# A decoder layer with expert retrieval: its token blocks regrouped from 1, 3 and 4 to 1, 2, 3 and 2, and its expert rows buffered one by one

## The chip, the cores and the metric

One core of a Trainium2 chip runs the whole kernel. The metric is device time in microseconds (us), the median of several executions.

## What is computed

A prompt of 1024 tokens and 8 sample tokens go through one layer, with all weights in float32:

```python
n = rmsnorm(x, g_mix) * (1 + sc1) + sh1
z = n @ w_in                                   # 1024 -> 4096
a_lin, a_gate, u, v, g_a, g_b = split(z)
a = a_lin * sigmoid(a_gate)
a = silu(layernorm(causal_dwconv(concat(hist, a), w_dw, b_dw))) @ w_conv_out    # 31 taps
v = layernorm(v, g_v, b_v)
b = (u * chunk_spatial_gate(v, w_s, b_s)) @ w_gmlp_out
m = sigmoid(g_a) * a + sigmoid(g_b) * b
x = x + gt1 * (m @ w_out)
n2 = rmsnorm(x, g_ffn) * (1 + sc2) + sh2
# expert retrieval, per token: 8 heads, 16 of 16384 experts each
q = n2 @ w_q
s1, s2 = q[:half] @ k1.T, q[half:] @ k2.T      # top 16 of 128 each, then top 16 of their sums
act = gelu(u_tab[eid] . n2)                    # 128 rows of 1024 per token
x = x + gt2 * sum(g * act * v_tab[eid])        # 128 more rows of 1024 per token
y = rmsnorm(x, g_final)
```

## The kernel before

The prompt is 8 blocks of 128 tokens; the 8 samples are a ninth, narrow block. The work on a block has two halves. The **front** is everything up to the expert ids and gates: norm, input projection, gated units, convolution, layer norms, the branch products, the output projection, second norm, query product, top 16 searches, and **routing** (`route`), which picks a block's 128 experts per token and turns them into ids (`eid`) and gates. The **expert half** is the gather: a block has 64 **pairs** of slots. For each slot of a pair GpSimd issues one indirect DMA (`fetch`) that brings for each of 128 partitions one expert's row of 2048 numbers, u and v together, so a pair moves 2 x 1 MB. VectorE multiplies the u half with the token's norm and sums (`dots`, L1507), ScalarE takes the gelu (L987), VectorE makes a 128 x 32 weight matrix of it (`weigh`, L1524), and TensorE adds the v half, weighted, into the block's sums (`value`, L765), after which `rows_used` gives the rows' buffer back to GpSimd. There are 516 pairs: 64 for each block, and 4 for the samples ahead of the last block.

**Groups.** Fronts are done for several blocks at once, since each reads all weights (in pieces of 1 MB through `wring`, a ring of 3 pieces, loaded by the sync engine in order, L403 to L409). Group 1 is block 0, group 2 blocks 1 to 3 (384 tokens), group 3 blocks 4 to 7 with the samples (520 tokens, in two halves of 260 columns). Group 1's front runs by itself. Group 2's runs beside the expert pairs 0 to 59 of block 0, group 3's beside the pairs 64 to 247. Each group's last `route` calls for its later blocks are done beside the pairs just before those blocks (`extra` in the VectorE program): 10 steps each, one step per pair.

**What sets the order.** Each engine's front is a generator that yields at fixed points. `front_weights` lists the same points with a weight each, `spread_front` deals them out over the pairs of a range in proportion, and `beside_peer` walks through the pairs on every engine: the pair's dots, a few front steps, the pair's weigh or value, the other front steps. At a range's last pair the rest of the generator is run to its end. TensorE does half of a pair's front steps ahead of its value. All engines work in this order, so a late step of the front holds back the value behind it.

```python
for g, lo, hi in ((G2, 0, END_B), (G3, PAIRS, END_C)):     # 0 to 60, 64 to 248
```

**Row buffers.** `buffer_plan` gives each pair a slot of two rows (16 KB per partition): three slots up to pair 255 (`WIDE_AT`), five after it, when parts of `big`, `w1` and `arena` that the fronts need have come free. GpSimd waits once per pair for the `rows_used` of the pair that had the slot.

Of the kernel before, what the change touches and what calls it, by code (L numbers as in the profile page):

```python
# [20 lines left out]
D = 1024  # L21
NP = 1024
NS = 8
# [5 lines left out]
W = 31  # L29
# [15 lines left out]
NB1 = 4  # L45
GW = 520
# [9 lines left out]
END_B = 60  # L56
END_C = 4 * PAIRS - 8
WIDE_AT = 4 * PAIRS
# [58 lines left out]
def build(nc, t):  # L117
# [3 lines left out]
    with ctx:  # L121
# [10 lines left out]
        big = sb("big", [P, 6 * 2 * D + KC * GW])  # L132
        nT = part(big, 6 * 2 * D, KC, GW)
# [3 lines left out]
        mbuf = sb("mbuf", [P, KC * GW])  # L137
        mT = part(mbuf, 0, KC, GW)
        wring = sb("wring", [P, RING * PIECE])

        AW = 512 + W - 1
        arena = sb("arena", [P, CC * (AW + 2 * GW) + 5 * DC])
        aT = part(arena, 0, CC, AW)
        yT = part(arena, CC * AW, CC, GW)
        v_tm = part(arena, CC * (AW + GW), 5, DC)
        uT = part(arena, CC * (AW + GW) + 5 * DC, CC, GW)
        ysq = part(arena, CC * (AW + GW), CC, GW)
        x_first = part(arena, CC * AW, 5, D)
        eq = part(arena, CC * AW + 5 * D, 2, TOP, NC)
        xn2 = part(arena, 3768, 5, D)  # L150
        xn1 = sb("xn1", [P, NB1, D])
        xr = sb("xr", [P, NQ, D])
        v16 = part(arena, 0, 5, NCH, TOP)
        i16f = part(arena, 5 * NCH * TOP, 5, NCH, TOP)
        i16 = i16f.bitcast(u32)
        rep = part(arena, 10 * NCH * TOP, 4, NKEY)
# [5 lines left out]
        rbc = w1[:, 2048:2048 + GW]  # L162
        xs = part(w1, 0, 2, D)
        qbuf = part(w1, 0, 2, GW)
        qs = part(w1, 2 * GW, NCH, NS)
        rep_s = part(w1, 2 * GW + NCH * NS, 4, NKEY)
# [45 lines left out]
        def row(r):  # L212
            if r < 8:
                return big[:, r * 2 * D:(r + 1) * 2 * D]
            return w1[:, 0:2 * D] if r == 8 else arena[:, 0:2 * D]
# [15 lines left out]
        S = {f"{n}{g}": ctx.enter_context(nc.semaphore(f"{n}{g}")) for n in group_names for g in (1, 2)}  # L231
        S |= {f"{n}{g}": ctx.enter_context(nc.semaphore(f"{n}{g}")) for n in ("x_in", "out_x1") for g in (1, 2, 3)}
# [6 lines left out]
        s_row = [ctx.enter_context(nc.semaphore(f"rows{i}")) for i in range(10)]  # L239
# [5 lines left out]
        def group(n, blocks, tg, xn, tables):  # L245
# [6 lines left out]
            g.S = {k: S[f"{k}{1 if n < 3 else 2}"] for k in group_names}  # L252
            g.S |= {k: S[f"{k}{n}"] for k in ("x_in", "out_x1")}
            g.base = totals(G1) if n == 2 else {}

            g.order = list(range(g.nb)) if n < 3 else [0, 1, 2, 4, 3]
            g.cand = part(tables, 0, g.nb * H, NC)
            g.cid = part(tables, g.nb * H * NC, g.nb * H, NC)
            g.posf = part(mbuf, 3200, g.nb * H, TOP) if n < 3 else part(mbuf, 0, g.nb * H, TOP)
            g.crep = part(mbuf, 3200 + 512, H, NC) if n < 3 else part(mbuf, 1024, H, NC)  # L260
            g.eq = eq if n < 3 else part(mbuf, 2048, 2, TOP, NC)
            g.gt1 = (gt1_a, gt1_b, gt1_c)[n - 1]
# [5 lines left out]
        GROUPS = (G1, G2, G3)  # L268
        before = {2: G1, 3: G2}

        def cols(b):
            i = 0 if b == 0 else b - 1 if b < NB1 else b - NB1
            return slice(i * P, i * P + width(b))
# [115 lines left out]
        def x1_again(b):  # L389
            return mbuf[:, b * D:(b + 1) * D] if b < NB1 else wring[:, (b - NB1) * D:(b - NB1 + 1) * D]  # L390
# [1301 lines left out]
```

## Time and profile before

| what | value |
|---|---|
| median of 3 runs | 3551.34 us (3548.37 to 3553.54) |
| the profiled execution | 3556.78 us |
| its span | 3555.2 us |
| TensorE busy | 2051.7 us (58%) |
| VectorE busy | 2448.6 us (69%) |
| GpSimd busy | 1249.4 us (35%) |
| ScalarE busy | 441.8 us (12%) |
| DMA | 1232.08 MB, mean 347 GB/s |

Shares of busy time are means over stretches with different limits, so the span has to be cut. The page's 40 slices show where the limits change, and windows cut at chosen pairs measure each stretch. A stretch in which the DMAs are full can't be made shorter by faster engines; one in which they are not is paced by the engine that the others wait for.

### The profile page before, as it was taken

Reading aid. Unit: us, or ns where it says so; the run is one execution under the profiler, and the core shown is the slowest. Engines: PE = TensorE matmul, PEld = TensorE weight load, DVE = VectorE, ACT = ScalarE, POOL = GpSimd, SP = SyncE. Lnnn points to the kernel's source line nnn. Section 1 sums busy time; section 2 is a strip of 40 time slices with the busy share of each in tenths; the row PEclk is TensorE's granted clock in tenths of the full one; section 3 lists DMA queues with packets and bytes.
Section 4 is the critical chain, followed back from the end, with each engine's and each line's share of the span. In section 5 each row is a group of like instructions: output and inputs, shape, how many; then the busy total and the mean of one; then the engine's idle time right before and its main releaser. Section 6 shows DMA issues by size and latency. Waiting matters only on the chain. (4 is left out here: it accounts for less than half of the span.)

```text
span 3555.2 us, 28830 instructions
## 1 busy us (share of the span) xinstructions
PE 2051.7 (58%) x9548; PEld 995.9 (28%) x9548; DVE 2448.6 (69%) x6290; ACT 441.8 (12%) x1031; POOL 1249.4 (35%) x1046
## 2 busy tenths in 40 slices
PE   6873878986277777778688623333343333355333
PEld 4762444643144344455345300000000000000000
DVE  1447574479898796655768997766866697656665
ACT  1121101011111110110211011101010101011100
POOL 0001221222233433333434334544454444445343
PEclk9886988998588888899799855555555555555555
DMA  7734756798579999899999869999999998998998
GB/s 297 311 144 166 301 207 260 272 358 318 220 283 360 363 334 371 329 383 419 395 410 406 345 251 401 375 422 422 368 417 421 422 386 354 421 421 341 423 421 343
DMA packets 183925, 1232.08 MB, mean 347 GB/s; under 512 B 30512, under 2 KB 31152, under 8 KB 36320
## 3 DMA queue, kind: packets, MB, share of 16 engines
q0 software_dynamic: 148608, 1082.20, 75.9%
q1 hardware_dynamic: 35168, 148.05, 10.6%
q8 instruction: 75, 1.23, 0.1%
q14 instruction: 74, 0.61, 0.0%
HBM read 1221.14 MB, written 9.02 MB: 346 GB/s over the span
## 5 line engine op out<-in xcount | busy, mean ns | idle before, releaser
L1045 POOL DMA_INDIRECT big<-in_experts,eid x920 | 1112.0, 1209 | 2081.9 <-PE ps L765 1620.4
L1507 DVE SCALAR_TENSOR_TENSOR big<-big,xr 128x1024 f32<-128x1024 f32 x920 | 1113.6, 1225 | 525.3 <-DMA big<-in_experts,eid 520.2
L765 PE MATMUL ps<-big,wd 128*32 128x512 f32 x3680 | 726.2, 873 | 1089.8 <-DVE wd L1524 1085.2
L530 PE MATMUL ps<-big,wring 128*128 128x260 f32 (+2 forms) x2400 | 644.9, 423 | 81.5 <-issue 56.3
L530 PEld LDWEIGHTS ps<-big,wring 128*128 128x128 f32 x2400 | 447.6, 201 | 318.7 <-issue 166.1
L765 PEld LDWEIGHTS ps<-big,wd 128*32 128x32 f32 x3680 | 85.0, 127 | 1591.0 <-DVE wd L1524 1535.7
L987 ACT ACTIVATE gel<-act 128x2 f32<-128x2 f32 x516 | 105.7, 205 | 2569.9 <-DVE big L1507 2322.8
L1524 DVE TENSOR_SCALAR wd<-mask,gel,gate 128x32 f32<-128x32 f32 x1024 | 275.1, 363 | 152.3 <-ACT gel L987 141.5
L765 PE MATMUL ps<-w,wd 128*32 128x512 f32 x208 | 100.3, 1061 | 174.7 <-DVE wd L1524 170.8
L1205 DVE SCALAR_TENSOR_TENSOR arena<-arena,wdw 128x128 f32<-128x128 f32 (+2 forms) x360 | 182.9, 572 | 0.0
L682 PE MATMUL ps<-wring,mbuf 128*128 128x256 f32 (+1 forms) x528 | 128.6, 400 | 11.6 <-DMA wring<-in_w_out 6.3
L682 PEld LDWEIGHTS ps<-wring,mbuf 128*128 128x128 f32 (+1 forms) x528 | 96.0, 186 | 54.7 <-issue 28.8
L530 PE MATMUL ps<-arena,wring 128*128 128x260 f32 (+1 forms) x384 | 107.1, 422 | 0.0
L1045 POOL DMA_INDIRECT w<-in_experts,eid x52 | 57.2, 1100 | 130.3 <-PE ps L765 126.3
L765 PE MATMUL ps<-arena,wd 128*32 128x512 f32 x208 | 100.3, 1061 | 0.0
L1507 DVE SCALAR_TENSOR_TENSOR arena<-arena,xr 128x1024 f32<-128x1024 f32 x52 | 63.7, 1226 | 50.6 <-DMA arena<-in_experts,eid 50.6
L765 PEld LDWEIGHTS ps<-w,wd 128*32 128x32 f32 x208 | 10.2, 140 | 264.8 <-DVE wd L1524 259.2
L530 PEld LDWEIGHTS ps<-arena,wring 128*128 128x128 f32 x384 | 71.5, 190 | 37.9 <-issue 15.1
L1507 DVE SCALAR_TENSOR_TENSOR w<-w,xr 128x1024 f32<-128x1024 f32 x52 | 63.7, 1225 | 19.8 <-DMA w<-in_experts,eid 19.5
L1507 DVE DVE_READ_ACCUMULATOR big<-big,xr 128x1 f32 x920 | 76.8, 84 | 0.0
L1045 POOL DMA_INDIRECT arena<-in_experts,eid x52 | 68.6, 1319 | 15.9 <-issue 15.9
L814 ACT ACTIVATE xr<-arena 32x1024 f32<-32x1024 f32 x64 | 67.5, 1055 | 1.5
(219 smaller groups left out, 1881.0 us busy)
## 6 DMA issues: line engine op xcount, KB each, us to landing
wring<-in_w_in SPq DMA_DIRECT2D x40, 1024.0 KB
wring<-in_w_q SPq DMA_DIRECT2D x19, 1024.0 KB
big<-in_experts,eid POOLq DMA_INDIRECT x920
wring<-in_w_ada SPq DMA_DIRECT2D x12, 1024.0 KB
wring<-in_w_out SPq DMA_DIRECT2D x9, 1024.0 KB
big<-in_w_ada SPq DMA_DIRECT2D x6, 1024.0 KB, 6.9
xr<-in_w_ada SPq DMA_DIRECT2D x6, 1024.0 KB, 8.8
big<-in_w_in SPq DMA_DIRECT2D x4, 1024.0 KB, 14.7
```

The source lines that it names most:

```text
L530: mm = mmul(out, piece(n)[:, c, col:col + P], src[:, c, gi * tg:(gi + 1) * tg], start=(c == 0), stop=(c == k - 1))
L682: mm = mmul(ps[0:w, 2 + i % 6, 0:256], mT[:, c, cols(b)], piece(n + col)[:, c, :], start=(c == 0), stop=(c == KC - 1))
L765: mm = mmul(ps[QUAD * j:QUAD * (j + 1), half, :], wd[:, 2 * (at % 4) + jj, :], row(2 * slot + jj)[:, D + 512 * h:D + 512 * (h + 1)], start ...
L814: made = ac(xr[QUAD * q:QUAD * (q + 1), j, :], xn[QUAD * j:QUAD * (j + 1), :], ACT.Copy)
L987: ac(gel[:, c:c + 2], act[:, c:c + 2], ACT.Gelu).then_inc(S["gelu"], 1)
L1045: gp.indirect_dma_start(row(r), None, t["experts"], bass.IndirectOffsetOnAxis(ap=index, axis=0)).then_inc(s_row[r], 16)
L1205: ins = v.scalar_tensor_tensor(out=y, in0=aT[:, c, kk:kk + g.np], scalar=wdw[:, c, kk:kk + 1], in1=y, op0=ALU.mult, op1=ALU.add)
L1507: last = v.scalar_tensor_tensor(out=row(r)[:, 0:D], in0=row(r)[:, 0:D], scalar=1.0, in1=x, op0=ALU.mult, op1=ALU.mult, accum_out=act[:, c: ...
L1524: last = v.tensor_scalar(wd[:, c, :], mask[:], gel[:, c:c + 1], gate[:, b % 4, 2 * half + jj, m:m + 1], ALU.mult, ALU.mult)
```

## The change

- The groups are now blocks 0; 1 and 2; 3 to 5; 6, 7 and the samples (`STARTS`). There is a fourth front, so all weights of a front are read once more. Each later front works on one column range: 256, 384 and 264 tokens.
- The fronts run beside pairs 0 to 59, 64 to 187 and 204 to 311 (`FRONT_AT`). The later routes run beside pairs 64 (group 2's), 192 and 202 (group 3's), 320 and 384 (group 4's: the samples' first, then block 7).
- The rows are kept singly: seven up to pair 319, ten after it. Each fetch waits for the pair that last used its own row. The seventh row is a tile of its own (`row7`), for which `mbuf` shrinks from 4160 to 3200 numbers.
- The tables, views and copies of x follow (group 3's x is loaded in group 2's time; blocks 3 to 5 are kept in `xn1`); the semaphores of the groups are shared by all, with a base count for each.

```diff
-NB1 = 4
-GW = 520
+STARTS = [0, 1, 3, 6]
+NB1 = STARTS[-1]
+NBL = NBT - NB1
+GT = (NBL - 1) * P + NS
+GX = 3 * P
+ROWS_1, ROWS_2 = 7, 10
+LAST = len(STARTS)
...
-END_B = 60
-END_C = 4 * PAIRS - 8
-WIDE_AT = 4 * PAIRS
+FRONT_AT = {2: (0, PAIRS - 4), 3: (PAIRS, 3 * PAIRS - 4), 4: (3 * PAIRS + 12, 5 * PAIRS - 8)}
+WIDE_AT = 5 * PAIRS
...
-    plan, uses, newest = [], [0] * 5, [None] * 5
+    plan, uses, newest = [], [0] * ROWS_2, [None] * ROWS_2
     for at in range(NPAIRS):
-        free = range(3 if at < WIDE_AT else 5)
-        slot = min(free, key=lambda i: -1 if newest[i] is None else newest[i])
-        plan.append((slot, uses[slot], newest[slot]))
-        uses[slot] += 1
-        newest[slot] = at
+        tiles = []
+        for _ in range(2):
+            free = range(ROWS_1 if at < WIDE_AT else ROWS_2)
+            r = min(free, key=lambda i: -1 if newest[i] is None else newest[i])
+            tiles.append((r, uses[r], newest[r]))
+            uses[r] += 1
+            newest[r] = at
+        plan.append(tiles)
...
-        big = sb("big", [P, 6 * 2 * D + KC * GW])
+        big = sb("big", [P, 6 * 2 * D + KC * GX])
...
+        row7 = sb("row7", [P, 2 * D])
+        mbuf = sb("mbuf", [P, 3200])
...
-        G1 = group(1, [0], P, xn1[:, 0:1, :], mbuf)
-        G2 = group(2, [1, 2, 3], 3 * P, xn1[:, 1:4, :], mbuf)
-        G3 = group(3, list(range(NB1, NBT)), 260, xn2, wring)
+        for n in range(1, LAST):
+            blocks = list(range(STARTS[n - 1], STARTS[n]))
+            GROUPS.append(group(n, blocks, len(blocks) * P, xn1[:, blocks[0]:blocks[-1] + 1, :], mbuf))
+        GROUPS.append(group(LAST, list(range(NB1, NBT)), GT, xn2, wring))
...
+        routing = [(PAIRS, ROUTE_PIECES, G2, 1), (3 * PAIRS, ROUTE_PIECES, G3, 1),
+                   (3 * PAIRS + ROUTE_PIECES, ROUTE_PIECES, G3, 2), (5 * PAIRS, ROUTE_PIECES + 1, G4, 1),
+                   (6 * PAIRS, ROUTE_PIECES, G4, 2)]
...
-                if earlier is not None:
-                    pool.wait_ge(S["rows_used"], earlier + 1)
                 for jj in range(2):
+                    r, _, earlier = PLAN[at][jj]
+                    if earlier is not None:
+                        pool.wait_ge(S["rows_used"], earlier + 1)
```

GpSimd's queue at its first fetches (`big` holds six rows, `row` is the seventh). Before:

```order
L1045 DMA big<-in_experts,eid 128x2048 [waits first_ids]
L1045 DMA big<-in_experts,eid 128x2048 x5
L1045 DMA big<-in_experts,eid 128x2048 [waits rows_used]
L1045 DMA big<-in_experts,eid 128x2048
L1045 DMA big<-in_experts,eid 128x2048 [waits rows_used]
L1045 DMA big<-in_experts,eid 128x2048
L1045 DMA big<-in_experts,eid 128x2048 [waits rows_used]
L1045 DMA big<-in_experts,eid 128x2048
```

and now:

```order
L1076 DMA big<-in_experts,eid 128x2048 [waits first_ids]
L1076 DMA big<-in_experts,eid 128x2048 x5
L1076 DMA row<-in_experts,eid 128x2048
L1076 DMA big<-in_experts,eid 128x2048 [waits rows_used] x7
L1076 DMA row<-in_experts,eid 128x2048 [waits rows_used]
L1076 DMA big<-in_experts,eid 128x2048 [waits rows_used]
L1076 DMA big<-in_experts,eid 128x2048 [waits rows_used,first_ids]
L1076 DMA big<-in_experts,eid 128x2048 [waits rows_used] x5
```

Every fetch has a wait of its own, seven are issued before the first of them, and the two fetches of a pair no longer wait for the same pair.

TensorE in block 0, at the third and the later pairs of group 2's input projection (four L765 rows are a pair's value; `wring` holds the weight pieces). Before:

```order
L530 MATMUL ps<-big,wring 128x384 x24
L765 MATMUL ps<-big,wd 32x512 x4
L530 MATMUL ps<-big,wring 128x384 x12
L765 MATMUL ps<-big,wd 32x512 x4
L530 MATMUL ps<-big,wring 128x384 x16
L765 MATMUL ps<-big,wd 32x512 x4
L530 MATMUL ps<-big,wring 128x384 x12
L765 MATMUL ps<-big,wd 32x512 x4
```

and now, with the line numbers of the new file (L562 and L797 are L530 and L765):

```order
L562 MATMUL ps<-big,wring 128x256 x16
L797 MATMUL ps<-big,wd 32x512 x4
L562 MATMUL ps<-big,wring 128x256 x16
L797 MATMUL ps<-big,wd 32x512 x4
L562 MATMUL ps<-big,wring 128x256 x8
L797 MATMUL ps<-big,wd 32x512 x4
L562 MATMUL ps<-big,wring 128x256 x12
L797 MATMUL ps<-row,wd 32x512
```

About as many matmuls lie beside each pair as before, but each has 256 columns instead of 384.

TensorE around pair 256. Before, 20 pairs of values follow each other behind the end of group 3's front (its last row is L736), and more after them:

```order
L736 MATMUL ps<-ident,mod 8x128 x8
L765 MATMUL ps<-big,wd 32x512 x80
L765 MATMUL ps<-w,wd 32x512
L765 MATMUL ps<-arena,wd 32x512
L765 MATMUL ps<-w,wd 32x512
```

and now group 4's output projection lies between them (L714; the rows with 8 are the samples'):

```order
L701 MATMUL ps<-ident,mod 8x128
L797 MATMUL ps<-row,wd 32x512
L797 MATMUL ps<-big,wd 32x512
L797 MATMUL ps<-row,wd 32x512
L797 MATMUL ps<-big,wd 32x512
L714 MATMUL ps<-wring,mbuf 128x256 x12
L797 MATMUL ps<-big,wd 32x512 x4
L714 MATMUL ps<-wring,mbuf 128x256 x4
L714 MATMUL ps<-wring,mbuf 8x256 x4
L797 MATMUL ps<-big,wd 32x512 x4
L714 MATMUL ps<-wring,mbuf 8x256 x4
```

The values of block 4's pairs stand behind front work as those of the blocks before do.

## Rows read from the trace of the kernel before

**Rows 1.** The page: 40 slices of 88.9 us, busy tenths, clock, DMA share, GB/s
```profile
PE   6873878986277777778688623333343333355333
DVE  1447574479898796655768997766866697656665
PEclk9886988998588888899799855555555555555555
DMA  7734756798579999899999869999999998998998
GB/s 297 311 144 166 301 207 260 272 358 318 220 283 360 363 334 371 329 383 419 395 410 406 345 251 401 375 422 422 368 417 421 422 386 354 421 421 341 423 421 343
```

**Rows 2.** Windows at pairs: start, 0, 60, 64, 84, 232, 248, 256, 272, 320
```profile
core 0: us, PE busy (x) PEld busy (x) DVE busy (x) ACT busy (x) POOL busy (x), PEclk, DMA share, GB/s
...
304.60:914.30 609.70, 465.27 (x1824) 262.30 (x1824) 406.02 (x1160) 71.95 (x152) 142.52 (x120) 0.87 0.70 268
914.30:932.40 18.10, 6.27 (x28) 0.81 (x32) 11.44 (x25) 0.82 (x4) 6.84 (x6) 0.50 0.60 226
932.40:1092.00 159.60, 101.59 (x444) 61.13 (x440) 145.66 (x405) 22.78 (x53) 50.80 (x40) 0.75 0.74 282
1092.00:1994.80 902.80, 690.84 (x3360) 425.89 (x3353) 656.06 (x1591) 131.19 (x320) 355.84 (x297) 0.87 0.96 381
1994.80:2128.00 133.20, 42.63 (x206) 14.30 (x204) 126.79 (x494) 11.80 (x27) 42.88 (x34) 0.56 0.73 280
2128.00:2164.80 36.80, 14.00 (x60) 1.61 (x64) 23.55 (x50) 5.87 (x12) 19.04 (x18) 0.50 0.81 329
2164.80:2255.70 90.90, 30.48 (x128) 3.02 (x120) 81.86 (x212) 6.16 (x19) 39.24 (x31) 0.50 0.92 370
2255.70:2497.00 241.30, 93.29 (x388) 9.87 (x392) 146.44 (x291) 26.63 (x64) 115.05 (x98) 0.50 1.01 422
```

**Rows 3.** Groups of instructions, TensorE, 304.6 to 914.3 us: busy, mean ns, idle before
```profile
L530 PE MATMUL ps<-big,wring 128*128 128x384 f32 x704 | 248.8, 507 | 37.8 <-issue 18.6 <-DVE arena L1253 8.0 <-DMA wring<-in_w_in 7.2
L765 PE MATMUL ps<-big,wd 128*32 128x512 f32 x480 | 71.7, 673 | 93.5 <-DVE wd L1524 92.3 <-DVE xn L1341 1.0
```

**Rows 4.** Who waited for whom: GpSimd in 304.6 to 914.3, then 932.4 to 2128 us
```profile
POOL big L1045 <- PE ps L765: 429.2, 57, 25.5
...
POOL big L1045 <- PE ps L765: 659.6, 177, 17.8
```

**Rows 5.** Windows as above: a busy TensorE, the wait for weights, a routing burst
```profile
388.00:427.00 39.00, 39.00 (x166) 24.12 (x165) 29.66 (x62) 2.57 (x8) 15.22 (x10) 1.00 0.87 340
1525.00:1537.00 12.00, 0.06 (x1) 0.09 (x1) 4.18 (x9) 1.65 (x3) 0.00 (x0) 0.57 1.02 423
1537.00:1560.00 23.00, 23.00 (x108) 15.76 (x109) 9.77 (x22) 4.45 (x8) 8.73 (x8) 0.93 0.73 272
1601.30:1633.30 32.00, 26.21 (x120) 17.40 (x120) 13.29 (x28) 2.63 (x6) 9.00 (x8) 0.82 1.02 417
2096.00:2128.00 32.00, 1.94 (x8) 0.20 (x8) 31.04 (x54) 4.14 (x5) 3.05 (x2) 0.50 0.39 158
```

**Rows 6.** Timeline of GpSimd: start, duration, idle before: first, last of twelve, 23.5
```profile
964.17 0.94 POOL L1045 DMA_INDIRECT big<-in_experts,eid  x1 [8.02 <-PE ps L765]
...
2106.65 2.11 POOL L1045 DMA_INDIRECT big<-in_experts,eid  x1 [10.90 <-PE ps L765]
...
2133.49 0.94 POOL L1045 DMA_INDIRECT big<-in_experts,eid  x1 [23.49 <-PE ps L765]
```

**Rows 7.** Groups by form, VectorE, whole span: the convolution taps
```profile
L1205 DVE SCALAR_TENSOR_TENSOR arena<-arena,wdw 128x512 f32<-128x512 f32 x120 | 84.6, 748 | 0.0
L1205 DVE SCALAR_TENSOR_TENSOR arena<-arena,wdw 128x384 f32<-128x384 f32 x120 | 66.0, 614 | 0.0
L1205 DVE SCALAR_TENSOR_TENSOR arena<-arena,wdw 128x128 f32<-128x128 f32 x120 | 32.3, 355 | 0.0
```

**Rows 8.** Windows as above: pairs 320 to 335 with one route, 336 to 383
```profile
2497.00:2586.50 89.50, 30.52 (x128) 3.02 (x120) 81.92 (x213) 6.16 (x19) 38.93 (x31) 0.50 0.91 364
2586.50:2827.20 240.70, 93.25 (x388) 9.89 (x392) 146.40 (x291) 26.64 (x64) 114.78 (x98) 0.50 1.01 422
```

**Rows 9.** The page: the DMA queue of the sync engine, packets, MB, share
```profile
q1 hardware_dynamic: 35168, 148.05, 10.6%
```

More of the change, by code:

```diff
@@ L238, in build @@
         s_piece = [ctx.enter_context(nc.semaphore(f"piece{i}")) for i in range(RING_1)]
-        s_row = [ctx.enter_context(nc.semaphore(f"rows{i}")) for i in range(10)]
+        s_row = [ctx.enter_context(nc.semaphore(f"rows{i}")) for i in range(ROWS_2)]
         def width(b):
@@ L443, in _ @@
                         sp.dma_start(xn1[:, b, :], t["x"][b * P:(b + 1) * P, :]).then_inc(S["x_in2"], 16)
[L444 removed]
+            for n in range(first_piece[2], first_piece[3]):
+                if n == first_piece[2] + 4:
+                    for b in G3.blocks:
+                        sp.dma_start(xn1[:, b, :], t["x"][b * P:(b + 1) * P, :]).then_inc(S["x_in3"], 16)
                 with_spill(n, G2)
[L447 removed]
@@ L746, in value @@
                 b, half, m = place(at)
-                slot = PLAN[at][0]
+                rows = [row(tile[0]) for tile in PLAN[at]]
                 pe.wait_ge(S["weights"], at + 1)
@@ L775, in sample_x @@
                     mm = mmul(ps[:, pair(k) + half, :], ident[0:NS, k:k + 1].broadcast_to([NS, P]),
-                              xn2[0:NS, 4, 512 * half:512 * (half + 1)], start=True, stop=True)
+                              xn2[0:NS, SB, 512 * half:512 * (half + 1)], start=True, stop=True)
                 mm.then_inc(S["xb_mm"], 1)
@@ L786, in begin @@
                         made[0] += 1
-            beside_peer(begin, value, {2: front(G2), 3: front(G3)}, lambda at: None, share=0.5)
+            beside_peer(begin, value, {g.n: front(g) for g in GROUPS[1:]}, lambda at: None, share=0.5)
         @block.scalar
@@ L966, in front @@
                     ac(gts, bank2(6)[0:NS, :], ACT.Copy).then_inc(s["gt_done"], 1)
-                yield from gap(27 if g.n == 3 else 11)
+                yield from gap(19 if g.n == LAST else 11)
                 next(g.numerators)
@@ L1001, in root @@
                 ac(stat[:, 1, lo:hi], stat[:, 0, lo:hi], ACT.Sqrt).then_inc(S["fin_root"], 1)
-            exps = {PAIRS + ROUTE_PIECES * i + 6: G2 for i in range(2)}
-            exps |= {at + 6: G3 for at in (4 * PAIRS, 5 * PAIRS, 6 * PAIRS, 6 * PAIRS + ROUTE_PIECES + 1)}
+            exps = {start + 6: g for start, _, g, _ in routing}
             copies = {half_start(h - 1) + 20 + c: (h, c) for h in range(2, 2 * NB) for c in range(8)}
@@ L1017, in extra @@
                     root(1, 0, NB)
-            beside_peer(gelu, lambda at: None, {2: front(G2), 3: front(G3)}, extra)
+            beside_peer(gelu, lambda at: None, {g.n: front(g) for g in GROUPS[1:]}, extra)
             square(NB)
@@ L1595, in to_slots, with later_routes @@
                 yield
-            def routing_2():
-                for i in (1, 2):
-                    yield from route(G2, i)
-            def routing_3():
-                for i in range(1, 4):
-                    yield from route(G3, i)
-                yield from to_slots()
-                yield from route(G3, 4)
-            second, third, norms = routing_2(), routing_3(), early_norm()
-            def extra(at):
-                if PAIRS <= at < PAIRS + 2 * ROUTE_PIECES:
-                    next(second, None)
-                for b, count in ((4, ROUTE_PIECES), (5, ROUTE_PIECES), (6, 2 * ROUTE_PIECES + 1)):
-                    if b * PAIRS <= at < b * PAIRS + count:
-                        next(third, None)
+            def later_routes():
+                for _, _, g, turn in routing:
+                    yield from route(g, turn)
+                    if g.blocks[g.order[turn]] == NB:
+                        yield from to_slots()
+            routes, norms = later_routes(), early_norm()
+            def extra(at):
+                for start, count, _, _ in routing:
+                    if start <= at < start + count:
+                        next(routes, None)
                 if at - 2 in ends:
@@ L1619, in _ @@
             dve.wait_ge(S["mask_made"], 1)
-            beside_peer(dots, weigh, {2: front(G2), 3: front(G3)}, extra)
+            beside_peer(dots, weigh, {g.n: front(g) for g in GROUPS[1:]}, extra)
             take_acc(2 * NB)
```

193 lines of the change are left out of this document (101 added, 92 removed).

## The prediction

> **What bounds the kernel now.** I read the page's slices first [rows 1]: no engine is full over the span. VectorE and TensorE are busy but gapped in the first half, and in the second half the DMA share stands at 0.9 to 1.0 with 421 GB/s. The windows, cut at the moments at which a named pair of slots begins its dot products, give each stretch its own limit [rows 2]. With no front beside them, pairs 272 to 319 take 241.3 us for 48, that is 5.03 each, at 422 GB/s: a pair gathers 2.1 MB, so this is the DMA's own pace, about 4.98 us, and a block of 64 pairs can't take less than 319 us. Above that floor lies all that a schedule can change:
>
> - Pairs 0 to 63, with group 2's front (384 tokens) beside 60 of them: 609.7 + 18.1 = 628 us, 309 over the floor. TensorE is busy for 465.3 of the 609.7 us and VectorE for 406.0, while the DMAs give 268 GB/s [rows 2]. The value matmuls take 71.7 of TensorE's time, the front the rest [rows 3], and GpSimd waits 429 us for TensorE to give rows back [rows 4]. So TensorE's order bounds this stretch.
> - Pairs 64 to 319, with group 3's front (512 tokens and the samples) beside pairs 64 to 247: 1564.6 us. The floor is 1275, and the front's 33.6 MB of weights are 80 us more at 421 GB/s, so 210 us are lost. They go where routing makes VectorE the slowest (159.6 us for the first 20 pairs, 133.2 for pairs 232 to 247), and where the front stops for something [rows 2]. From the start to pair 0's dots, 304.6 us, nothing changes.
> - From pair 320, 2497 us, 1058 us to the end, mostly the floor.
>
> **What a stop costs.** In pairs 151 to 154 TensorE waits 14 us for two weight pieces. While it waits the DMAs run at 423 GB/s, so nothing is lost yet; the loss comes behind it, 23 us at 272 GB/s, since no rows had been given back. That is 8 us of DMA time [rows 5]. The routing burst at a front's last pair is larger: VectorE has 31 us of work in pair 247, and the DMAs fall to 158 GB/s for 32 us, 20 us lost; GpSimd stands still for 23.5 us in it [rows 5, 6].
>
> **The change part by part, against the profiled 3556.8 us (span 3555.2; the median of the runs is 5.4 lower).**
>
> 1. *Group 2 shrinks from three blocks to two.* In block 0, TensorE's front work goes to two thirds: 394 to 263 us, and with 72 us of values 335 instead of 465. The 144 us in which it idled are kept (479 us for 60 pairs) or shrink alike (431). But the DMAs now matter: 60 × 4.98 + 80 = 379 us, 6.3 per pair, so a light pair can no longer run at the 3 us of its dots. I went through the printed orders pair by pair, gave each instruction the mean duration of its form (half a matmul's time for half its columns), and added up, for each pair, the largest of TensorE's work, VectorE's work and the pair's DMA share. For the kernel before this gives 608 us where 609.7 were measured, so I go by it: after, it gives 507, and 20 for the last four pairs. **Block 0: 628 to 527, minus 101.** Ends: 449 and 560.
> 2. *Pairs 64 to 319 now hold two fronts*, group 3 with 384 tokens beside 124 pairs and group 4 with 256 and the samples beside 108. The columns that TensorE multiplies are the same as before, only moved, but three things are added. The weights are read once more: 80 us of DMA time in a stretch that is near the floor. The convolution's 120 tap instructions come once more: 614 and 748 ns for 384 and 512 columns [rows 7] make 163 us, and with groups of 256, 384 and 256 (a tap of 256 lies between the 355 and 614 ns of its neighbours, at 485) 190: 27 us more on VectorE. And the norms, softmax chains and burst at the end of a front come once more. The same pair-by-pair sum gives 1556 us for the kernel before (1564.6 measured) and 1708 after. **Plus 152.** From below: if the second front only cost its DMA time and took a third of block 0's work along, plus 80. From above: twice the 210 us lost now, and 80, plus 290.
> 3. *What such a sum can't see*: the two mid-branch waits for weight pieces in every front (8 us each, above) and the waits at its phase borders. Over group 3's front the measured time is 18 us above the sum (1195.6 against 1177). A third front repeats this: **plus 18** (0 to 40).
> 4. *Seven single row buffers beside the fronts instead of three pairs.* Half a pair more can be fetched before a stop empties the queue. The price is to be seen in routing: ten pairs of VectorE work at 7 us instead of 5 should cost 20 us, and do so with three pairs of buffers; with five they cost 10 (89.5 us against 16 × 4.98 = 80) [rows 8]. With three pairs of buffers the first 20 pairs of group 3's front, two routes among them, ran 51 us over their 5.42 each [rows 2]. So two pairs of buffers absorb 10 us, one row 2.5. Between pairs 64 and 247 GpSimd waits twelve times for over 8 us, the longest 17.8 [rows 4] but for the 23.5 above; I take these for nine stops, and 18 with two fronts: **minus 45**. In block 0 the rows wait for the engines anyway, and I take nothing. From below 0, from above 70 if block 0 gains too. Before, the waits for `rows_used` came once per pair; now each fetch has one, on an otherwise idle queue: nothing.
> 5. *Widening to ten rows at pair 320 instead of 256*: the two routes of group 3 (pairs 192 to 211) run with seven rows. This is inside term 2, which counts them at their full work.
> 6. *The end*: block 6 no longer holds two routes but one; by the same sum the rest from pair 320 to the last dots goes from 1035 to 1016: **minus 19**. The moved norm inputs, the smaller `mbuf` and the shared semaphores add no instruction on a path that is waited for: group 3's x is loaded one front ahead, and group 4's is asked for at group 3's last pair, 16 pairs before its use.
>
> Sum: −101 + 152 + 18 − 45 − 19 = **+5 us**. Carried to the median of the runs, 3551.3 + 5 = 3556.
>
> The Trainium skill (Perfetto Trace Analysis, Per-instruction lifecycle) says that VectorE's SBUF operations are slower than spec by a fixed cost per instruction, so that small operands suffer most. It speaks against smaller groups; the taps agree (355 ns at 128 columns, 748 at four times as many), and term 2 already pays it.
>
> **The rivals.**
>
> *Faster: block 0 shrinks in full.* Block 0 is where most was lost, and term 1's lower end is 78 us below what I take. If TensorE's idle shrinks with its work, the end is at 3556 − 78 = 3478. For it: GpSimd's 429 us of waiting there are all for TensorE [rows 4]. Against: where TensorE works without a gap (39 us at full clock), the DMAs already give 340 GB/s [rows 5]; with a third less work beside each pair they are the next bound.
>
> *Slower: the third front costs as much as the second did.* Its place is pairs 204 to 311, of which pairs 272 to 311 ran at 5.03 us with VectorE 61 per cent busy [rows 2]. My sum has 728 us for these 108 pairs, 6.7 each, 110 over gathers and weights (108 × 4.98 + 80 = 618). If group 4's front loses there what group 3's did, the 210 us less some 40 for two routes, the end is 60 later, at 3616. It decides from 7.3 us per pair. For it: bursts and waits for pieces come once per front, not per token. Against: group 3's front with twice the tokens ran at 6.5 per pair, routes included.
>
> *The seventh buffer does nothing.* In the wait for weights above the DMAs were full. A further gather in flight then only stands before the weights, and TensorE starts 2.5 us later for each row that came 2.5 us sooner. Then term 4 is nought: 3601. The Trainium skill (Trainium Kernel Development and Optimization, Key Constraints) says that DMAs issued from SP, ACT and POOL all run on the same 16 engines and interleave. By that rule the gathers and weights do delay each other, and the trace agrees: 417 GB/s together in a window with both [rows 5]. But behind such a wait the DMAs run dry, and there the row counts.
>
> **How the numbers follow.** A measurement can tell some 0.2 per cent, 7 us, from no change. The balance as summed: 0.50, 3520 to 3595 where each term errs by a fifth, of which 0.18 lie faster, 0.16 within 7 us, 0.16 slower. Block 0 in full: 0.27. The full third front: 0.12. The idle seventh row: 0.11. So faster 0.45, same 0.16, slower 0.39. The predicted time is the balance's, 3556. The range goes from the fast rival, 3475, to above the slow one, 3625; what lies outside are sums in which two rivals meet.
>
> **What would show it.** In the windows after: pair 64 begins its dots near 830 us instead of 932, and pair 320 near 2515 instead of 2497. Weight bytes rise by 33.6 MB, on a queue that moves 148 MB now [rows 9]; if not, the change doesn't do what it says. TensorE's busy time stays near 2050 us, VectorE's goes up by 30 to 40. DMA slices between 2160 and 2500 us fall from 420 to 340 GB/s. The stops of 14 us for weight pieces stand six times, not four. I'd be wrong by term 1 if block 0 ends before 790, by term 2 if pairs 64 to 319 take less than 1630 us or more than 1740, and by term 4 if pairs in routing bursts still lose what they did.

## The result and the profile after

| | kernel before | changed kernel |
|---|---|---|
| median, 14 runs each on one chip | 3547.64 us (3533.81 to 3553.54) | 3558.63 us (3547.98 to 3564.04) |
| ratio | 1 | 1.0033, 95% interval 1.0021 to 1.0045 |
| the profiled execution, its span | 3556.78, 3555.2 us | 3552.07, 3550.0 us |
| TensorE, VectorE busy | 2051.7, 2448.6 us | 2049.4, 2470.4 us |
| DMA | 1232.08 MB | 1264.60 MB |
| bytes on the sync engine's queue, which loads the weights | 148.05 MB | 180.56 MB |

The changed kernel is slower by 0.33 per cent, 11 us. The time that I named, 3556 us, is 2.6 us off, but it stood for a difference of 5 us, inside what a measurement can tell from no change, and the measured one lies 4 us outside (its interval is 7 to 16 us). The profiled executions scatter by more than this effect (by the two in the table the changed kernel would be 5 us faster, and a second profile of it has a span of 3569.9 us), so they are used for where the time lies, and the medians for how much it is.

The page of the changed kernel, slices of 88.8 us, its clock, DMA share and GB/s, and the sync engine's queue:

```profile
PE   6864877935867786862376677672343333354333
...
DVE  1456864798796556798968655689866585657665
...
PEclk9976988956978897975587888785555555556555
DMA  7836887968998899997779989995999999999998
GB/s 290 324 133 233 352 310 306 397 272 330 388 358 341 314 401 421 399 387 308 283 298 394 370 350 420 405 408 215 406 409 421 422 373 420 421 421 364 423 422 340
...
q1 hardware_dynamic: 39488, 180.56, 12.8%
```

Against the kernel before [rows 1], the fifth to ninth slices, in block 0, have risen from a mean of 280 GB/s to one of 327 (four of the five rose, the ninth fell), and the stretch near the floor now begins at the 29th slice instead of the 25th. Between 2160 and 2500 us there is a fourth front, with one slice at 215 GB/s, its last burst.

Windows of the changed kernel, cut at pairs 0, 60, 64, 192, 248, 256, 304, 320, 384, 448 and the end:

```profile
298.90:793.50 494.60, 345.87 (x1656) 236.80 (x1656) 348.64 (x996) 60.98 (x145) 136.69 (x117) 0.82 0.80 317
793.50:813.60 20.10, 8.21 (x36) 1.01 (x40) 12.09 (x26) 1.46 (x5) 10.79 (x10) 0.50 1.01 414
813.60:1657.90 844.30, 590.41 (x2376) 282.56 (x2368) 639.79 (x1686) 111.94 (x247) 304.43 (x256) 0.81 0.90 362
1657.90:2050.80 392.90, 222.59 (x988) 116.93 (x988) 315.25 (x775) 55.41 (x119) 140.64 (x112) 0.72 0.88 345
2050.80:2103.00 52.20, 38.76 (x177) 26.60 (x174) 26.99 (x59) 7.36 (x17) 14.58 (x14) 0.85 0.83 323
2103.00:2393.40 290.40, 217.67 (x1084) 127.07 (x1083) 204.29 (x608) 35.95 (x105) 112.24 (x98) 0.86 1.00 409
2393.40:2512.00 118.60, 29.67 (x132) 3.34 (x136) 105.32 (x359) 15.37 (x28) 38.20 (x35) 0.52 0.67 262
2512.00:2837.10 325.10, 123.77 (x516) 12.91 (x512) 224.23 (x480) 32.64 (x83) 152.04 (x128) 0.50 1.00 414
2837.10:3183.30 346.20, 129.12 (x525) 14.76 (x518) 228.56 (x503) 32.64 (x83) 153.79 (x130) 0.50 0.99 409
3183.30:3550.00 366.70, 152.07 (x572) 20.27 (x571) 230.36 (x446) 35.98 (x99) 157.98 (x126) 0.53 0.94 388
```

Block 0 took 514.7 us instead of 628 [rows 2], pairs 64 to 319 took 1698.4 instead of 1564.6, and from pair 320 to the end 1038 instead of 1058.2. So 113 us were won in block 0, 134 lost behind it, and 20 won at the end; the rest of the difference between the two profiles, 6 us, is the stretch before pair 0.

In finer stages (us between the dots of the pairs named, from the two profiles):

| pairs | before | after | what stands beside them now |
|---|---|---|---|
| 0 to 31 | 348 | 282 | group 2's projection and branches, 256 columns for 384 |
| 32 to 63 | 280 | 233 | its output projection, queries, routing |
| 64 to 187 | 818 | 829 | group 3's front, 384 columns for 512 |
| 188 to 203 | 86 | 95 | a route and the start of another, formerly front work |
| 204 to 311 | 620 | 740 | the rest of that route and group 4's front; formerly 44 pairs of front and a route |
| 312 to 319 | 41 | 35 | nothing |
| 320 to 383 | 330 | 325 | one route |
| 384 to the end of the last dots | 714 | 699 | one route instead of two |

Nearly all of the loss is in pairs 204 to 311. There the pace is 6.85 us per pair; the slow rival needed 7.3, my sum had 6.7.

The waits of the changed kernel, GpSimd for TensorE in block 0 and in pairs 64 to 319, then VectorE for rows in the latter stretch:

```profile
POOL big L1076 <- PE ps L797: 354.1, 56, 28.7
...
POOL big L1076 <- PE ps L797: 966.8, 239, 23.5
...
DVE big L1536 <- DMA big<-in_experts,eid: 316.4, 191, 13.4
```

GpSimd's waiting for TensorE beside pairs 0 to 59 fell from 429.2 us [rows 4] to 354.1, 75 us, while the stretch itself became 115 us shorter; the DMAs carry 317 GB/s there now instead of 268. Its longest wait behind block 0 is a routing burst of 23.5 us, exactly that of before [rows 6]:

```profile
2455.89 2.10 POOL L1076 DMA_INDIRECT big<-in_experts,eid  x1 [10.90 <-PE ps L797]
2458.30 0.94 POOL L1076 DMA_INDIRECT row<-in_experts,eid  x1 [0.30 <-issue]
2482.75 0.93 POOL L1076 DMA_INDIRECT big<-in_experts,eid  x1 [23.52 <-PE ps L797]
```

This is GpSimd's timeline at pair 311, group 4's last: the seventh row has been issued, at 2458.30, and the engine then waits as long as it did with six.

### The profile page after: what moved, and what is told of

Its sections match the earlier page's. It is cut to its first block, busy times and chain, and to the rows that moved or that the text cites. A ratio compares the mean times of both kernels' runs of the same rounds, so it can differ in the third digit from the quotient of the medians.

```text
span 3550.0 us, 29121 instructions
## 1 busy us (share of the span) xinstructions
PE 2049.4 (58%) x9564; PEld 1006.1 (28%) x9564; DVE 2470.4 (70%) x6457; ACT 449.5 (13%) x1042; POOL 1233.4 (35%) x1046
## 2 busy tenths in 40 slices
DMA packets 188247, 1264.60 MB, mean 356 GB/s; under 512 B 30992, under 2 KB 31632, under 8 KB 36544
## 3 DMA queue, kind: packets, MB, share of 16 engines
q1 hardware_dynamic: 39488, 180.56, 12.8%
## 4 chain that ended last, share of the span: by engine, by line
DMA 25%; DVE 13%; PE 9%; issue 5%; POOL 2%; ACT 1%; POOLq 0%; ACTq 0%; DVEq 0%
DMA big<-in_experts,eid 12%; DMA w<-in_experts,eid 12%; PE ps L562 4%; PE ps L797 4%; DVE big L1536 3%; POOL big L1076 2%; DVE wd L1553 2%; DVE eid_s L1499 1%; DVE mbuf L1497 1%; DVE arena L1497 1%; DVE arena L1494 1%; DVE mbuf L1494 1%; PE ps L807 1%; ACT gel L1019 1%; PE ps L714 0%
## 5 line engine op out<-in xcount | busy, mean ns | idle before, releaser
L1076 POOL DMA_INDIRECT big<-in_experts,eid x829 | 969.7, 1170 | 2178.2 <-PE ps L797 1754.3
L797 PE MATMUL ps<-big,wd 128*32 128x512 f32 x3316 | 806.9, 856 | 1039.3 <-DVE wd L1553 1035.3
L1536 DVE SCALAR_TENSOR_TENSOR big<-big,xr 128x1024 f32<-128x1024 f32 x829 | 1004.0, 1223 | 483.7 <-DMA big<-in_experts,eid 477.7
L562 PE MATMUL ps<-big,wring 128*128 128x256 f32 (+3 forms) x2400 | 671.3, 435 | 125.9 <-issue 79.9
L562 PEld LDWEIGHTS ps<-big,wring 128*128 128x128 f32 x2400 | 459.6, 206 | 381.0 <-issue 209.3
L797 PEld LDWEIGHTS ps<-big,wd 128*32 128x32 f32 x3316 | 94.0, 126 | 1529.8 <-DVE wd L1553 1472.1
L797 PE MATMUL ps<-row,wd 128*32 128x512 f32 x472 | 184.4, 869 | 127.0 <-DVE wd L1553 117.5
L1235 DVE SCALAR_TENSOR_TENSOR arena<-arena,wdw 128x256 f32<-128x256 f32 (+2 forms) x480 | 199.0, 478 | 0.0
L1536 DVE SCALAR_TENSOR_TENSOR row<-row,xr 128x1024 f32<-128x1024 f32 x118 | 144.1, 1221 | 58.1 <-DMA row<-in_experts,eid 57.6
L1076 POOL DMA_INDIRECT row<-in_experts,eid x118 | 147.0, 1245 | 36.0 <-issue 36.0
L714 PE MATMUL ps<-wring,mbuf 128*128 128x256 f32 (+1 forms) x528 | 130.9, 406 | 9.6 <-DMA wring<-in_w_out 6.5
L714 PEld LDWEIGHTS ps<-wring,mbuf 128*128 128x128 f32 (+1 forms) x528 | 98.3, 191 | 54.1 <-issue 27.3
L562 PE MATMUL ps<-arena,wring 128*128 128x256 f32 (+2 forms) x384 | 107.2, 422 | 0.0
L846 ACT ACTIVATE xr<-xn 32x1024 f32<-32x1024 f32 x96 | 101.1, 1053 | 2.0
L562 PEld LDWEIGHTS ps<-arena,wring 128*128 128x128 f32 x384 | 71.4, 190 | 37.4 <-issue 15.9
L797 PE MATMUL ps<-arena,wd 128*32 128x512 f32 x152 | 73.3, 1061 | 3.0 <-DVE wd L1553 3.0
L797 PEld LDWEIGHTS ps<-row,wd 128*32 128x32 f32 x472 | 20.9, 127 | 188.4 <-DVE wd L1553 160.9
L797 PE MATMUL ps<-w,wd 128*32 128x512 f32 x156 | 74.3, 1049 | 0.0
```

Source lines behind the costliest of these rows:

```text
L562: mm = mmul(out, piece(n)[:, c, col:col + P], src[:, c, gi * tg:(gi + 1) * tg], start=(c == 0), stop=(c == k - 1))
L714: mm = mmul(ps[0:w, 2 + i % 6, 0:256], mT[:, c, cols(b)], piece(n + col)[:, c, :], start=(c == 0), stop=(c == KC - 1))
L797: mm = mmul(ps[QUAD * j:QUAD * (j + 1), half, :], wd[:, 2 * (at % 4) + jj, :], rows[jj][:, D + 512 * h:D + 512 * (h + 1)], start=(m == 0), ...
L846: made = ac(xr[QUAD * q:QUAD * (q + 1), j, :], xn[QUAD * j:QUAD * (j + 1), :], ACT.Copy)
L1076: gp.indirect_dma_start(row(r), None, t["experts"], bass.IndirectOffsetOnAxis(ap=index, axis=0)).then_inc(s_row[r], 16)
L1235: ins = v.scalar_tensor_tensor(out=y, in0=aT[:, c, kk:kk + g.np], scalar=wdw[:, c, kk:kk + 1], in1=y, op0=ALU.mult, op1=ALU.add)
```

## The experiments

Each kernel was timed against the kernel before on the same chip; the kernels of one batch share its runs. The medians of the kernel before in the three batches are 3544.89, 3544.69 and 3545.74 us.

**The changed kernel again**, as the base of the first batch.

> The changed kernel once more, on the chip of the three beside it. Theory (the sum of the prediction): within 0.1 to 0.5 per cent slower than the kernel before, 3552 to 3565 us.

Measured: 3562.22 us (5 runs), ratio 1.0047 (1.0034 to 1.0061). Its stages agree with the first profile's within 8 us: block 0 took 520.6 us, pairs 64 to 319 1701.5, and the stretch from pair 320 to the end 1045.9. Below, the changed kernel stands as 3559 to 3562 us. Of the three batches it has runs in the first alone, so beside the kernels of the other two its ratios to the kernel before, 1.0033 and 1.0047, are the better base (a ratio and the quotient of the two medians differ by up to 0.0006).

**Six rows instead of seven**, the grouping alone:

```diff
-ROWS_1, ROWS_2 = 7, 10
+ROWS_1, ROWS_2 = 6, 10
```

> The changed kernel with six single row buffers beside the fronts instead of seven. My theory (a row absorbs 2.5 us of each of 18 stops): 45 us slower than the changed kernel, near 3603, all of it in pairs 64 to 319. Rival (the seventh buffer does nothing, since it only stands before the weights): within 7 us of the changed kernel.

Measured: 3642.73 us, ratio 1.0271 (1.0253 to 1.0290). The seventh row is worth 80 us by the medians and 65 to 85 by the profiles, and not 45. Windows of it, pairs 0 to 63 and 64 to 319, then 160 to 183, 184 to 191, 192 to 203:

```profile
302.10:839.30 537.20, 361.26 (x1692) 241.23 (x1696) 362.09 (x1020) 62.89 (x149) 142.32 (x126) 0.80 0.79 309
839.30:2594.70 1755.40, 1110.12 (x4752) 559.19 (x4748) 1293.95 (x3483) 225.97 (x516) 608.32 (x516) 0.77 0.88 346
...
1487.20:1644.70 157.50, 113.51 (x460) 52.40 (x460) 130.19 (x520) 13.99 (x40) 53.78 (x48) 0.80 0.91 350
1644.70:1713.40 68.70, 14.72 (x64) 1.62 (x64) 59.18 (x168) 8.72 (x15) 19.87 (x16) 0.50 0.65 258
1713.40:1793.20 79.80, 24.02 (x104) 2.41 (x96) 73.26 (x212) 5.31 (x15) 31.83 (x24) 0.50 0.83 323
```

and the last three stretches of the changed kernel:

```profile
1447.80:1592.00 144.20, 109.91 (x456) 52.12 (x460) 129.15 (x521) 14.03 (x40) 52.33 (x48) 0.83 0.96 389
1592.00:1657.90 65.90, 17.04 (x72) 1.62 (x64) 59.03 (x169) 8.79 (x16) 22.62 (x17) 0.50 0.67 262
1657.90:1737.70 79.80, 22.58 (x96) 2.43 (x96) 73.24 (x212) 5.31 (x15) 31.27 (x24) 0.50 0.84 334
```

Of the row's gain 17 to 22 us lie in block 0, where I had taken nothing, and 54 to 57 in pairs 64 to 319. Within those it isn't where I had put it. In pairs 160 to 183 it gains 13 us; in the routing burst and the route behind it, where I had read its price, 3 and 0. In pairs 160 to 183 a pair with 6.7 us of top 16 searches on VectorE is followed by one with 3.0 or 4.4, and TensorE's work too changes from pair to pair. Over the 24 pairs VectorE is busy for 129 us and TensorE for 110, both less than the 138 us for which the DMAs are busy (0.96 of 144.2), so it is the alternation that makes the DMAs wait. There the DMA share rises from 0.91 to 0.96. In the burst and the route behind it VectorE has more work than the DMAs for many pairs together (59 of 65.9 us and 73 of 79.8), and there one row more gained next to nothing. Nor did the row remove many stops: in pairs 64 to 319 GpSimd waits for over 8 us 29 times with six rows, and 27 and 28 times in the two profiles with seven.

What the row did take away are VectorE's waits for rows. With six, in pairs 0 to 63 and then 64 to 319:

```profile
DVE big L1536 <- DMA big<-in_experts,eid: 62.4, 37, 5.0
...
DVE big L1536 <- DMA big<-in_experts,eid: 389.2, 238, 11.2
```

and with seven, in the same two stretches (the last line is the seventh row's own):

```profile
DVE big L1536 <- DMA big<-in_experts,eid: 19.5, 20, 3.4
...
DVE big L1536 <- DMA big<-in_experts,eid: 316.4, 191, 13.4
DVE row L1536 <- DMA row<-in_experts,eid: 17.0, 14, 4.0
```

In pairs 64 to 319 these waits are 56 us shorter, as much as the stretch itself; in block 0 they are 43 us shorter, of which 17 to 22 show in the time.

**Five rows**, for the slope:

```diff
-ROWS_1, ROWS_2 = 7, 10
+ROWS_1, ROWS_2 = 5, 10
```

> The changed kernel with five single row buffers beside the fronts. My theory: each row less costs at least as much as the one before, so 100 us or more slower than the changed kernel. Beyond stops, five rows of 1 MB give 2.5 pairs in flight, and the loop of a pair took 18 us in pairs 128 to 191 of the kernel before, so 7.2 us per pair instead of 6.2 would give 250 us more. Rival: rows don't matter, below 30 us.

Measured: 3830.09 us, ratio 1.0805 (1.0791 to 1.0820), 268 to 271 us above the changed kernel. The sixth row is worth 187 us, the seventh 80. The expectation's 250 us, from the loop of a pair, came near: pairs 128 to 191 took 7.4 us each with five rows, where the loop gave 7.2, and 6.6 with six, 6.2 with seven.

**Rows kept singly in the kernel before**, six beside the fronts:

```diff
+ROWS_1, ROWS_2 = 6, 10
...
-        slot = min(free, key=lambda i: -1 if newest[i] is None else newest[i])
+            r = min(free, key=lambda i: -1 if newest[i] is None else newest[i])
...
-                if earlier is not None:
-                    pool.wait_ge(S["rows_used"], earlier + 1)
                 for jj in range(2):
+                    r, _, earlier = PLAN[at][jj]
+                    if earlier is not None:
+                        pool.wait_ge(S["rows_used"], earlier + 1)
```

> The kernel before with its six rows kept singly (and ten after pair 256), groups as they were. In even counts a pair's two rows still wait for the pair three ahead, so my theory: no change within 0.2 per cent. Rival (the single waits themselves help or cost on GpSimd): more than 7 us either way.

Measured: 3546.41 us (11 runs), ratio 1.0005 (0.9996 to 1.0014). Keeping rows singly does nothing by itself. The difference of the changed kernel is thus made of two parts: the groups, +98 us (3642.7 against 3544.9), and the seventh row, −80. The groups' part includes the widening to ten rows at pair 320 instead of 256, which no run takes out of it. The kernel before with a seventh row wasn't tried: the 8 KB per partition for the row are what `big` (4352 bytes) and `mbuf` (3840) give up with the narrower groups.

**The order of two weight pieces in every later front.** The sync engine loads the pieces in the order of their use. The twelfth and eighteenth of a front are the second output pieces of the two branches. Each has to wait for the ring place of a piece that TensorE uses long, the branch's first output piece, and the next input piece stands behind it in the queue, though its place is free sooner and it is wanted sooner. The two change places:

```diff
+            early = {}
+            for g in GROUPS[1:]:
+                for k in (11, 17):
+                    at = first_piece[g.n] + k
+                    early |= {at: at + 1, at + 1: at}
             def with_spill(n, g):
-                load(n)
+                load(early.get(n, n))
```

> The changed kernel, in whose later three fronts the sync engine loads the third input piece of a branch ahead of its second output piece, so that at mid-branch one piece of 1 MB is waited for and not two. Theory (term 3: a wait for pieces costs some 8 us of DMA time, six of them, half of each goes): 15 to 25 us faster than the changed kernel. Rival (these waits are covered by rows that wait for their dots anyway): within 7 us of the changed kernel (about 3560 us).

Measured: 3538.61 us (12 runs), ratio 0.9987 (0.9977 to 0.9997), 20 to 24 us below the changed kernel by the medians, 16 to 21 by the ratios. TensorE's waits ahead of its weight loads, of the changed kernel:

```profile
PEld ps L562 <- issue: 225.2, 187, 15.0
```

and with the order changed (L568 is the same line):

```profile
PEld ps L568 <- issue: 147.5, 189, 8.8
PEld ps L568 <- DMA wring<-in_w_conv_out: 28.4, 3, 9.6
PEld ps L568 <- DMA wring<-in_w_gmlp_out: 27.8, 3, 9.9
```

One of these stops, the second of group 3, in TensorE's timeline of the changed kernel and then of this one:

```profile
1222.60 5.14 PE L562 MATMUL ps<-big,wring 128*128 128x384 f32 x8 [13.72 <-issue]
...
1213.12 5.49 PE L568 MATMUL ps<-big,wring 128*128 128x384 f32 x8 [8.75 <-DMA wring<-in_w_conv_out]
```

In the changed kernel TensorE's weight loads stand for 12 to 15 us six times; now for 9 to 10, six times. The stretches with two such waits each are shorter by 8 to 10 us (pairs 16 to 31), 9 to 11 (96 to 127) and 9 to 10 (224 to 255), by the two profiles of the changed kernel. So a shortening of each wait by 2 to 6 us, 4.5 in the mean, was worth 3 to 5 us, at least the 3 us that 8 us for a full wait of 14 would give.

**Routing pieces spread out.** The ten route steps before each burst get more weight, so that the front's last pairs hold less:

```diff
-            yield from [1] * 4 + [2] * (28 if g.n == LAST else 20)
+            yield from [1] * 4 + [2] * (18 if g.n == LAST else 10) + [7] * 10
```

> The changed kernel with weights of 7 instead of 2 for the last ten steps of each front, which are the route of its first block, so that the route takes nearly one pair per step instead of falling into the last two. Theory (a burst of 31 us costs 20 us of DMA time, spread over ten pairs it costs 10 less): 20 to 35 us faster than the changed kernel. Rival (what the burst gives back is lost where the front's other steps are pressed into fewer pairs): within 10 us, or slower.

Measured: 3567.59 us, ratio 1.0069 (1.0055 to 1.0083), 5 to 9 us slower than the changed kernel. The tails gain, pairs 160 to 187 14 us and 288 to 311 16 to 17, but the front's other steps are pressed into fewer pairs: by the two profiles of the changed kernel pairs 0 to 59 lose 9 to 15 us, 64 to 127 16 to 19, and 248 to 255 10 to 11. The burst is a place where the loss shows, not work that can be had for nothing.

**Both edits together**, the two diffs above:

> Both edits in the changed kernel. Theory: the sum of the two, 35 to 60 us faster than the changed kernel, so faster than the kernel before by 0.7 per cent or more. Rival: no more than the larger of the two.

Measured: 3557.86 us, ratio 1.0037 (1.0023 to 1.0050), no better than the changed kernel. The 35 to 60 us expected did not come; the rival, no more than the larger gain, held. If a gain of 0.0046 to 0.0060 and a loss of 0.0022 to 0.0036 simply added up, the ratio would be 1.0009 to 1.0023. The measured one is 5 to 10 us above that, which the intervals can just cover, so whether the two hinder each other is open.

**Both edits in the kernel before:**

```diff
-            yield from [1] * 4 + [2] * (36 if g.n == 3 else 20)
+            yield from [1] * 4 + [2] * (26 if g.n == 3 else 10) + [7] * 10
...
-                load(n)
+                load(early.get(n, n))
```

> Both edits in the kernel before, with its groups and three pairs of buffers. It has two later fronts instead of three, so the theory gives two thirds: 23 to 40 us faster than the kernel before. Rival: its first front is so tight (60 pairs) that spreading costs there what it gives, below 10 us.

Measured: 3524.93 us (6 runs, 3523.57 to 3528.76), ratio 0.9950 (0.9936 to 0.9964): 20 us under the kernel before, less than the 23 to 40 expected, and the fastest version of all that computes the whole layer. It beats both kernels. The next two take it apart.

**The order of the pieces alone in the kernel before**, the same diff as above:

> The kernel before with only the order of the loads swapped. Theory (the swap gave 20 us with three later fronts): 13 us faster than the kernel before (9 to 18), so two thirds of what both edits gave there (20). Rival: all 20 are the swap's, and the spread gives nothing.

Measured: 3532.67 us (12 runs), ratio 0.9965 (0.9951 to 0.9980), minus 13. Four such waits stand in that kernel against six in the changed one, and two thirds of 20 are 13.

**The order, and a milder spread (weight 4):**

```diff
-            yield from [1] * 4 + [2] * (36 if g.n == 3 else 20)
+            yield from [1] * 4 + [2] * (26 if g.n == 3 else 10) + [4] * 10
```

> The kernel before with the swap, and with weights of 4 instead of 7 for the last ten steps of each front (2 in the kernel before). Theory (half the spread takes the tip off the burst and presses the rest less): 20 to 30 us faster than the kernel before. Rival: between the two others, 13 to 20.

Measured: 3534.99 us (12 runs), ratio 0.9964 (0.9949 to 0.9979). That is no gain over the order alone; whether the 7 us that weight 7 has beyond them are the spread's can't be settled, as they come from different batches and the intervals overlap.

**A smaller fourth front's weights.** Group 4 loads an eighth of each of its weight pieces; everything else runs as it was, on the numbers that lie in the ring:

```diff
-                sp.dma_start(home(n), src[col]).then_inc(s_piece[slot_of[n]], 16)
+                cut = 256 if first_piece[4] <= n < first_piece.get(5, len(pieces)) else PIECE
+                sp.dma_start(home(n)[:, 0:cut], src[col][:, 0:cut]).then_inc(s_piece[slot_of[n]], 16)
```

> The changed kernel, in which group 4's front (beside pairs 204 to 311) loads only an eighth of each of its 32 weight pieces, so that its products use what an earlier piece left there. All instructions stay. It takes 29 MB off the DMAs, 70 us at 421 GB/s. My theory (term 2: the extra weights cost their DMA time, since the stretch is near the DMAs' pace, and the waits for pieces go too): 60 to 85 us faster than the changed kernel (3560), all of it in pairs 204 to 311, so the grouping's loss is mainly the third reading of the weights. Rival (VectorE's and TensorE's work set the pace of this front, and the weights fit beside): below 35 us.

Measured: 3509.24 us (4 runs), ratio 0.9900 (0.9873 to 0.9927), 49 to 53 us below the changed kernel. The window of pairs 204 to 311, of the changed kernel:

```profile
1737.70:2477.30 739.60, 472.12 (x2224) 269.90 (x2220) 555.16 (x1537) 102.92 (x242) 255.57 (x218) 0.78 0.90 357
```

and with an eighth of the weights:

```profile
1737.10:2428.30 691.20, 466.20 (x2224) 268.51 (x2220) 553.50 (x1536) 103.24 (x242) 254.62 (x218) 0.80 0.88 344
```

The whole gain lies here: 48 us, of the 70 that seven eighths of 33.6 MB take at 421 GB/s. TensorE and VectorE do the same work in less time. So about 0.7 of a front's weight reading is on the path, and the third reading costs some 55 to 60 us (an estimate: 8/7 of the 48 to 53). That is between the expectation's 60 to 85 and its rival's 35. The waits for pieces did not go with the bytes, as expected: TensorE's two mid-branch stops in this front shrank from 14.6 and 13.4 us to 10.7 and 8.8. Wrong products may also pick other experts for group 4's blocks, but that changed no time: block 6's pairs, 384 to 447, took 345.9 us (346.2 in the changed kernel). The Trainium skill (Trainium Kernel Development and Optimization, Key Constraints) says that DMAs issued from SP, ACT and POOL run on the same 16 engines and interleave; if nothing else held the stretch up it would be all 70 by that, and the measured 48 says that a third of them is hidden. The other 60 or so of the 120 us that pairs 204 to 311 lost aren't the bytes of the weights.

**The same for group 2**, `first_piece[2]` and `first_piece.get(3, ...)` in that line:

> The same for group 2's front, beside pairs 0 to 59. My theory (term 1: with two blocks in the group the DMAs are as much a bound as TensorE): 30 to 60 us faster than the changed kernel, in block 0. Rival (TensorE's order alone bounds block 0, with two blocks as with three): below 15 us.

Measured: 3534.48 us (10 runs), ratio 0.9966 (0.9951 to 0.9981), 24 to 28 us below the changed kernel, of the same 70, and between the two expectations. In the profiles 12 to 14 us of it lie in pairs 16 to 31. Somewhat over a third of what these bytes take shows in the time; for the rest of block 0 something else sets the pace, and by the waits above that is the order of TensorE, as before.

## Why the prediction came out as it did

The time and the balance were right, in part by luck: two terms were too small, the loss behind block 0 (+170 forecast, +191 measured) and the gain of the seventh row (−45 forecast, −80 measured).

1. *Block 0, minus 101.* With six rows it is −91 (537.2 against 627.8), with seven −107 to −113. The sum of each pair's largest work, calibrated on the kernel before, was 10 us too low. Two things kept block 0 in the range and away from the fast rival (−179): TensorE's front work fell by a third, but it idled 149 us beside pairs 0 to 59 (494.6 less 345.9) as it had 144, and the DMA share rose to 0.80. "If TensorE's idle shrinks with its work" is what didn't happen. Pair 64 began at 814 us where I said 830: with six rows it began at 839, the row took 17 to 22 off, and the stretch before pair 0 was 6 us shorter in this profile.
2. *Pairs 64 to 319, plus 152, and 3. plus 18.* With six rows the stretch takes 1755.4 us, 191 more than before, where these terms have 170. The weights are not the undersized part: they cost some 55 to 60, and 80 is their DMA time. The waits for pieces came six times, as said, and their price stood the test of the swapped order in both kernels. My sum for pairs 204 to 311 was 728 us, and it was calibrated on six rows: with six 764.2 were measured, 36 more, and with seven 740. So this stretch is where the term was too small; some 16 of the 36 are its two waits for pieces, which term 3 counts. The slow rival needed 788, which neither count of rows reached. That group 4's 264 columns leave TensorE less to do in each pair may be why; no run shows it.
3. *The seventh row (term 4), minus 45.* This is the step that failed: its size by the medians is −80. "Two pairs of buffers absorb 10 us, one row 2.5", read from routing, times 18 stops, was the wrong rule in the wrong place. The experiment with six rows shows nothing or 3 us in routes and bursts, while pairs 160 to 183, where light and heavy pairs alternate, gained 13; "in block 0 the rows wait for the engines anyway" failed too: VectorE waited 62 us for rows there with six and 19 with seven. I had said that term 4 is wrong if routing bursts still lose what they did. They do: the wait at the last is 23.5 us as before. The rival in which the seventh row does nothing fell with it.
4. *The end, minus 19.* Measured −20, by the second profile −12, with six rows −18.
5. *Rows kept singly, nothing.* Measured +1.5 us, with an interval of −1 to +5.

Together: −91 + 191 − 18 = +82 by profiles for the groups (+98 by medians; the profiled execution of the kernel before was 12 us above its batch's median, that with six rows 6 below), −65 to −85 for the row. I had −101 + 170 − 19 = +50 and −45. Each was undersized by 20 to 50 us, and the errors cancelled; a balance of two large numbers came within 6 to 12 us (+11 and +17 were measured for +5) by luck as well as by sums. That the result lies on the slow side of the bound of 7 us is not something that such a sum can decide: the slower cases had 0.39 of the chance.

Of the other signs: the bytes on the sync engine's queue rose by 32.5 MB (33.6 named), TensorE stayed at 2049 us, VectorE rose by 22 us (30 to 40 named). The DMA slices between 2160 and 2500 us did not go down evenly to 340 GB/s: they are 420, 405, 408 and 215, a mean of 362. VectorE's taps, by form, are

```profile
L1235 DVE SCALAR_TENSOR_TENSOR arena<-arena,wdw 128x256 f32<-128x256 f32 x240 | 99.9, 477 | 0.0
L1235 DVE SCALAR_TENSOR_TENSOR arena<-arena,wdw 128x384 f32<-128x384 f32 x120 | 66.8, 610 | 0.0
L1235 DVE SCALAR_TENSOR_TENSOR arena<-arena,wdw 128x128 f32<-128x128 f32 x120 | 32.3, 347 | 0.0
```

so 477 ns at 256 columns where I had put 485, and 199 us for all where the kernel before had 183 [rows 7]. That is 16 us more where I had 27, since I multiplied means: 240 taps of 477 ns would be 114 us, and the row is busy for 99.9, because each tap's record overlaps the next one's. It is part of why VectorE rose by less than named. The fixed cost per instruction that the Trainium skill names (Perfetto Trace Analysis, Per-instruction lifecycle) shows again, since 128 columns more cost some 130 ns and the first 128 cost 347.

What stays open is what makes up the 60 us in pairs 204 to 311 that aren't the weights' bytes. VectorE is busy there for 555 us where the kernel before had 493, and TensorE for 472 where it had 300: the stretch holds front work that lay elsewhere, and the norms, softmax chains and burst once more. By my terms the waits for pieces are some 16 of the 60, and with an eighth of the bytes they were still 19.5 of their 28 us long. No run took one of these out.

## What to carry to other kernels

A schedule of alternating steps can be forecast from the order alone: for each step add up every engine's work and the DMA's share, take the largest, and sum, if the same sum reproduces the kernel that was measured. Here it gave −101 for a measured −91 and, with the stops that it can't see, +170 for +191. What such a sum leaves out is how much unevenness the buffers in flight absorb, and this has to be measured, by taking one buffer away from the kernel that runs (the first row taken away cost 80 us, the second 187), not read from a stop. In this kernel a buffer evened out steps that alternate (13 us in 24 pairs) and did next to nothing where one engine was the slowest throughout (3 us in 20 pairs). In a ring filled in order, look for a load that waits for its place while the next one is wanted sooner; exchanging two of them took 13 us off the kernel before.

## What the runs showed that I had not expected

The value of a 1 MB row in flight is large and falls steeply: 5, 6 and 7 rows gave 3830, 3643 and 3562 us, although TensorE and VectorE were busy for no more than 58 and 70 per cent of the span. And an eighth of a front's weights, which TensorE multiplies in the same time, made TensorE's own stretch 48 us shorter: a third of what the weights take at 421 GB/s is hidden, not all and not none.
